# Keys of the sample caches one sequence further ahead, norm weights on the activations, and row statistics for x

## The reference, cut to what matters

```
h = x
layer 0: xn = rms_norm(h, g_norm[0]);  u, v, gate = split(xn @ w_in_a)
         v = layer_norm(v);  s = spatial(v)
         h += (u * s * silu(gate)) @ w_out_a
every layer i: h += (p[i] @ w_ple[i]) * sigmoid(rms_norm(h, g_ple[i]) @ w_ple_gate[i])
         k, v = split(rms_norm(h, g_kv) @ w_kv)
layer 1: xn = rms_norm(h, g_norm[1]);  q, gate = split(xn @ w_in_b)
         h += (stick_breaking(q, k, v and the paged cache) * silu(gate)) @ w_out_b
y = rms_norm(h, g_final)
rms_norm(x, g) = x / sqrt(mean(x * x) + eps) * g
```

## Time and profile before

| | |
|---|---|
| median of 3 runs | 1244.79 us (1242.97 to 1245.74) |
| the profiled execution, its own time | 1243.67 us |
| its span in the profile | 1241.9 us |
| mean granted TensorE clock | 0.931 of full speed |
| busy: PE, PEld, DVE, ACT, POOL | 1150.2, 1007.1, 608.0, 438.4, 358.1 us |
| HBM read, written | 103.53 MB, 6.95 MB |

### The profile page before, as it was taken

The page is one execution under the profiler, slowest core; times in us unless marked ns, Lnnn a source line. Parts: engine busy times, 40 slices in busy tenths (PEclk is TensorE's granted clock), DMA queues, the critical chain, the costliest instruction groups (busy, mean ns, idle before and its releaser), DMA issues.

```text
span 1241.9 us, 20511 instructions
## 1 busy us (share of the span) xinstructions
PE 1150.2 (93%) x7950; PEld 1007.1 (81%) x7950; DVE 608.0 (49%) x869; ACT 438.4 (35%) x685; POOL 358.1 (29%) x262
## 2 busy tenths in 40 slices
PE   7899799999999897998999999999988868799797
PEld 6899699999999897997877778787646546489796
DVE  5655445533455444555666666665443212233443
ACT  5111235431343323233455546545533212122321
POOL 6422166522365146462111111100001000005542
PEclk9999899999999998999999999999957877779899
DMA  8222122233222422213122121121315564712201
GB/s 228 83 68 84 51 69 68 85 97 94 72 68 68 120 85 68 68 52 87 51 69 69 51 66 53 51 68 34 115 46 203 176 231 172 242 53 79 68 1 72
DMA packets 148264, 111.23 MB, mean 90 GB/s; under 512 B 3970, under 2 KB 138258, under 8 KB 148114
## 3 DMA queue, kind: packets, MB, share of 16 engines
q1 hardware_dynamic: 148210, 110.49, 28.9%
HBM read 103.53 MB, written 6.95 MB: 89 GB/s over the span
## 4 chain that ended last, share of the span: by engine, by line
PE 79%; DVE 6%; SPq 4%; DMA 3%; POOL 3%; issue 2%; ACT 2%; DVEq 0%; ACTq 0%; POOLq 0%
PE acc L1127 54%; PE zb L1296 4%; PE ob L1327 4%; DMA kpage<-in_cache_k_dram 3%; PE acc L1390 2%; PE zb L1312 2%; PE zb L1315 2%; PE acc L1280 2%; SPq L558 2%; PE zb L1250 1%; PE ob L1439 1%; POOL sumsq L704 1%; POOL raw L669 1%; PE acc L1161 1%; PE zb L1299 1%
## 5 line engine op out<-in xcount | busy, mean ns | idle before, releaser
L1127 PE MATMUL acc<-act_hi,w_hi 128*128 128x272 f32 x1904 | 403.5, 293 | 17.6 <-DVE gate L1744 9.1
L1127 PE MATMUL acc<-act_hi,w_lo 128*128 128x272 f32 x1904 | 398.2, 291 | 0.0
L1127 PE MATMUL acc<-act_lo,w_hi 128*128 128x272 f32 x1904 | 397.8, 291 | 0.0
L1127 PEld LDWEIGHTS acc<-act_hi,w_hi 128*128 128x128 f32 x1904 | 304.7, 191 | 24.0 <-issue 10.2
L1127 PEld LDWEIGHTS acc<-act_lo,w_hi 128*128 128x128 f32 x1904 | 304.1, 192 | 0.0
L1127 PEld LDWEIGHTS acc<-act_hi,w_lo 128*128 128x128 f32 x1904 | 302.6, 192 | 0.0
L669 POOL TENSOR_TENSOR raw<-raw,cols 128x1024 f32<-128x1024 f32 x96 | 194.0, 2031 | 295.4 <-DMA raw<-in_w_in_b_dram 114.9
L838 ACT ACTIVATE w_hi<-raw 128x1024 fp32r<-128x1024 f32 x120 | 126.4, 1055 | 224.3 <-PE acc L1127 143.9
L1537 DVE TENSOR_TENSOR w_lo<-raw,w_hi 128x1024 fp32r<-128x1024 f32 x120 | 168.6, 1406 | 68.5 <-ACT w_hi L838 68.0
L1767 DVE TENSOR_SCALAR relz<-zb,bias 128x128 f32<-128x128 f32 (+1 forms) x64 | 35.2, 550 | 97.1 <-ACT absz L983 97.1
L983 ACT ACTIVATE absz<-zb,bias 128x128 f32<-128x128 f32 (+1 forms) x64 | 33.7, 526 | 121.4 <-PE zb L1299 121.3
(11 more groups left out here) (234 smaller groups left out, 1322.3 us busy)
## 6 DMA issues: line engine op xcount, KB each, us to landing
raw<-in_w_in_a_dram SPq DMA_DIRECT2D x48, 512.0 KB, 4.0
kpage<-in_cache_k_dram SPq DMA_DIRECT2D x32, 512.0 KB, 5.8
vpage<-in_cache_v_dram SPq DMA_DIRECT2D x32, 512.0 KB, 5.1
raw<-in_w_out_a_dram SPq DMA_DIRECT2D x16, 512.0 KB, 4.0
raw<-in_w_ple_gate_dram SPq DMA_DIRECT2D x16, 512.0 KB, 3.9
raw<-in_w_kv_dram SPq DMA_DIRECT2D x16, 512.0 KB, 3.9
raw<-in_w_in_b_dram SPq DMA_DIRECT2D x16, 512.0 KB, 4.0
raw<-in_w_out_b_dram SPq DMA_DIRECT2D x8, 512.0 KB, 5.6
```

What stands on the lines that cost most here:

```text
L1127: mm = pe.matmul(t[:, c, 0:TH], wt[:, s, kt, :], xt[:, kt, c * TH:(c + 1) * TH], start=start and kt == kts[0] and wt is w_hi and xt is xh, ...
```

## The change

Three parts.

**Sample loads.** SP now loads the keys of b before the values of b-1. Each load keeps its own wait.

**Norm weights.** `g_norm[0]` and both `g_ple` no longer multiply the panels on POOL, but the activations: ACT's `act_hi` takes a scale, DVE's `act_lo` becomes one scalar_tensor_tensor (h * g - act_hi). Only the 32 panels of `w_kv` and `w_in_b` are still scaled on POOL, since these two share one set of activations and differ in their weight; for the rest ACT waits for the DMA itself.

**Start.** The mean squares of x come from batch-norm statistics on DVE (rows of `x_nat`, mean squared plus variance), with Ln, Exp and Newton on 5 columns instead of 544. The inverse roots become diagonal matrices `diag`, which PE spreads with ones to `rinv` after the first value panel. ACT, not DVE, copies the turned x into `h`. The transposes of `ws_nat` move behind the first group of value panels.

```diff
-            for b in range(2, NB):
-                sp.wait_ge(keyed, (b - 1) * KEYS)
-                load_keys(b)
-                sp.wait_ge(v_full, (b - 1) * 2)
-                load_values(b)
+            for b in range(2, NB + 1):
+                if b < NB:
+                    sp.wait_ge(keyed, (b - 1) * KEYS)
+                    load_keys(b)
+                if b > 2:
+                    sp.wait_ge(v_full, (b - 2) * 2)
+                    load_values(b - 1)
...
+        def scaled(p):
+            return END_PL0 <= p < END_B + AHEAD
...
             for n in range(KT):
                 squares(n)
-                scale_next()
...
-                act.wait_ge(raw_scaled, panel.now(1))
+                if scaled(panel.before + panel.here):
+                    act.wait_ge(raw_scaled, panel.now(1 - END_PL0))
+                else:
+                    act.wait_ge(raw_in[s], panel.lap(SLOTS) * 16 + 16)
...
+                    nc.scalar.activation(act_hi[into][:, sl(n), :], h[:, sl(n), :], ACT.Identity,
+                                         scale=gain[:, sl(n)]).then_inc(x_hi, 1)
...
+                    dve.scalar_tensor_tensor(one(act_lo[into]), one(h), gain[:, sl(n)],
+                                             one(act_hi[into]).bitcast(F32), ALU.mult, ALU.subtract).then_inc(x_lo, 1)
...
+            for t in range(TT):
+                act.wait_ge(turned, t + 1)
+                n = P if t < QB else NS
+                nc.scalar.activation(h[:, :, tokens(t)].rearrange("p (a b) t -> p a b t", a=2),
+                                     acc[t % 2][:, :, :].rearrange("p a (b t) -> p a b t", t=P)[:, :, :, 0:n],
+                                     ACT.Copy).then_inc(h_in, 1)
+            accs.step(TT + 1)
+            split_next()
+            act.wait_ge(x_mean, 1)
+            nc.scalar.activation(ln_s[:, 1, :], ln_s[:, 0, :], ACT.Ln).then_inc(x_root, 1)
+            act.wait_ge(x_root, 1)
+            nc.scalar.activation(ln_s[:, 1, :], ln_s[:, 1, :], ACT.Exp, scale=-0.5).then_inc(x_root, 1)
...
+            value_tiles(0)
+            for half in range(2):
+                t = turn()
+                dve.tensor_copy(ws_t[:, half * (NG // 2):(half + 1) * (NG // 2), :], t[:, 0, :]).then_inc(acc_read, 1)
```

More of the change, by code:

```diff
@@ L667, in scale @@
                     pool.engine_nop().then_inc(raw_scaled, 1)
-                else:
-                    pool.tensor_tensor(raw[:, s, :, :], raw[:, s, :, :], gain[:, :, None].to_broadcast([P, KT, P]),
-                                       ALU.mult).then_inc(raw_scaled, 1)
+                    panel.step()
+                    return
+                pool.tensor_tensor(raw[:, s, :, :], raw[:, s, :, :], gain[:, :, None].to_broadcast([P, KT, P]),
+                                   ALU.mult).then_inc(raw_scaled, 1)
                 panel.step()
             def scale_next():
-                if panel.reg is None and panel.now() >= END:
-                    return
                 p = panel.before + panel.here
+                assert scaled(p)
                 if panel.reg is not None:
@@ L721, in _ @@
                 .then_inc(bs_ready, 1)
-            turns[0] = N_AV // SLOTS - 1
-            with repeat(pool, turns[0], (panel, SLOTS)):
-                for k in range(SLOTS):
-                    scale_next()
-            for k in range(SLOTS):
-                scale_next()
             pool.wait_ge(vout_step, 1)
@@ L748, in turn @@
                         pool.tensor_tensor(s_t[:, :], u_r[:, :], g_r[:, :], ALU.mult).then_inc(y_made, 1)
-                turns[0] = N_UG // SLOTS - 1
-                with repeat(pool, turns[0], (panel, SLOTS), (ytile, 2)):
+                with repeat(pool, N_UG // SLOTS, (ytile, 2)):
                     turn()
-                turn()
             mix(0)
-            for n in range(KT):
-                scale_next()
             mix(1)
@@ L770, in embed @@
                 squares(KT - 1, True)
-            embed()
+            panel.step(END_PL0)
+            embed(0)
             turns[0] = NP - 1
@@ L778, in _ @@
                     scale_next()
-            for k in range(4):
+            for _ in range(AHEAD + 1):
                 scale_next()
@@ L1555, in turn, with lo_x @@
                 return t
-            def lo_x(n, into, src=None):
+            def lo_x(n, into, src=None, gain=None):
                 xt.step()
@@ L1619, in _ @@
+            dve.scalar_tensor_tensor(ln_s[:, 0, :], ln_s[:, 0, :], EPS, mv[:, :, 1], ALU.add, ALU.add)\
+                .then_inc(x_mean, 1)
+            turns.step(TT)
+            accs.step(TT)
             t = turn()
             dve.tensor_copy(cols[:, :], t[:, 0, 0:N_COL]).then_inc(acc_read, 1)
-            lo_tokens(QB)
             split_next()
-            for half in range(2):
-                t = turn()
-                dve.tensor_copy(ws_t[:, half * (NG // 2):(half + 1) * (NG // 2), :], t[:, 0, :]).then_inc(acc_read, 1)
+            dve.wait_ge(x_root, 2)
@@ L1626, in _ @@
+            newton(ln_s[:, 1, :], ln_s[:, 0, :], ln_s[:, 2, :])
+            for c in range(TT):
+                n = P if c < QB else NS
+                ins = dve.tensor_scalar(diag[0:n, c, 0:n], ident[0:n, 0:n], ln_s[0:n, 1, c:c + 1], None, ALU.mult)
+            ins.then_inc(diag_set, 1)
+            for n in range(KT):
+                lo_x(n, 0, None, g_norm_c[0])
             for _ in range(AHEAD - 1):
                 split_next()
-            rms()
-            with repeat(dve, N_AV // SLOTS, (panel, SLOTS), (done, SLOTS), (accs, 2 * SLOTS), (turns, SLOTS)) as i:
+            dve.wait_ge(rinv_full, 1)
```

136 lines of the change are left out of this document (70 added, 66 removed).

## The result

| | before | after |
|---|---|---|
| median | 1243.88 us (1242.04 to 1245.74, 4 runs) | 1192.49 us (1191.33 to 1193.57, 4 runs) |
| span of the profiled execution | 1241.9 us | 1191.2 us |
| mean granted TensorE clock | 0.931 | 0.951 |

The changed kernel takes 0.9587 of the time, 95% interval 0.9568 to 0.9605: 51.4 us less. 1192 us was predicted.

A forecast was written before the change was run, and what follows sets the result against it. PE was taken as the bound, busy 1150.2 of 1241.9 us, with gains left only in sample steps, out-panel ends and start. 35.9 + 13.4 + 3.5 = 52.8 off 1243.67 gave 1190.9, plus 1.1 for the median: 1192 us, range 1185 to 1207.

The forecast's parts named there:

- Sample steps: Five steps from 969.33 to 1072.83 us: all five waits for keys go, steps take 13.5 us, 35.9 us less.
- The ring through SP's queue: In the sample steps: product, four loads of values, four loads of keys, transposes, product; the change takes the values out.
- The rival of a DMA bound of 14.7 us: Sample steps: loads can't overlap, steps last 14.7 us instead of 13.5, 6 us less gain, 1198 us; chance 0.15.
- Norm weights: Ends of the two out-panel stages: without POOL's scaling PE resumes earlier, twice 6.7, so 13.4 us less.
- 8.61 - 0.9: Panel after the wait at an out-panel stage's end: 8.61 us before, 0.9 us taken back, between 0 and 2.58.
- everything between the ends at nothing: Between the stages' ends, POOL's scalings lay beside PE's full stretches, so their absence was costed at nothing.
- "some 5 us" of the last part: Ends of both out-panel stages, among the signs to look for: Ln comes some 5 us after the last block.
- Start: First panel at about 17.8 us, second group at 54.0 instead of 58.50: 3.5 us less, between 0 and 6.
- loses about 1 us: Second group of value panels at the start: after the new wait for a PSUM tile, about 1 us of clock lost.
- The clock stays low in the steps: Sample steps: the waits go but the clock stays low, 21.3 us less instead of 35.9, 1207 us; chance 0.12.
- the slower case: Sample steps: PE runs at the 1.2 GHz level through all five, 25.4 us a step, 1251 us; chance 0.02.
- a full recovery at the ends: Out-panel ends: clock recovers wholly, 1.7 twice, and the start gains its upper bound, 2.5: 1186 us; chance 0.08.

The follow-up runs named there:

- loads_alone: The kernel before with only the new order of the page loads: 1206.97 us, 0.9707.
- filled_waits: The kernel before, old order of loads, with 13 extra identity matmuls on PE in each of sample steps 1 to 5, during the waits for keys: 1233.65 us, 0.9925.
- light_steps: The changed kernel with less PE work in the sample steps (half the key transposes and most cumulative sums left out from the third sequence): 1180.8 us, one run.
- copies_first: The changed kernel with DVE's two copies of ws_t moved ahead of the five statistics of the first group of values: 1185.57 us, 0.9542.
- gate_panels_alone: The kernel before with only the gate panels' norm weights moved to the activations; POOL still passes each panel on by a nop: 1232.84 us, 0.9911.
- busy_waits: copies_first plus extra identity matmuls at PE's waits at the start, in the gate stages and before the first turn of keys: 1174.6 us, 0.9449.
- busy_no_tail: busy_first_gap without the added matmuls of the last two sample steps: 1165.05 us, 0.938.
- busy_attention: busy_waits plus 20 short unused matmuls per block on PE in the prompt's last attention passes: 1172.62 us, 0.942.
- busy_tail: busy_attention plus short unused matmuls in the last two sample steps, in place of the key transposes: 1170.76 us, 0.9423.
- busy_start: The changed kernel with 14 extra identity matmuls on PE between the transposes of x and the first panel: 1192.44 us, 0.9588.
- busy_first_gap: busy_tail plus 27 more short unused matmuls in the first wait of the last attention passes: 1167.53 us, 0.9385.

## Why the prediction was right, point by point

The total was right to 0.5 us, and that close only by luck. The parts summed to 52.8 us, the spans differ by 50.7, since 2.8 us were lost and 1.6 gained in places that the sum left out, the start gave 1.3 less and the norm weights 0.5 more. Of the 2 us that this makes, the choice of runs gave 1.5 back: the forecast added 1.1 us for the median over the profiled execution, and the changed kernel's median came out 0.4 below its own profiled one.

**Sample steps: right, 35.9 against 35.8.** The ring through SP's queue was the cause, the step came out as composed from rows of before, 13.55 against 13.5, and loads_alone gave 36.3 by itself. That the clock is part of it is shown by filled_waits (about 11 us), and that the waits alone are not the price also: they were 21.3. The rule of the Trainium skill that stood beside that term ("TensorE: Matmul & The Clock Gate", section "HAM oscillation — how this bites in real kernels") holds here, in waits of 3.2 to 5.3 us with the transposes at 3.67 us or so behind each. The rival of a DMA bound of 14.7 us falls with the steps of 13.55, and light_steps has no wait for a page at a mean of 12.4.

**Norm weights: right, 13.4 against 13.9** (7.1 and 6.8). Blocks 6.01 us apart, Ln 6.1 us after the last block (471.79 to 477.85), against 6.3 in the sum (474.2 to 480.5; the "some 5 us" of the last part was loose). The panel after the wait took 7.79 us where I had 8.61 - 0.9 = 7.7; that this term fits is in part luck, since the same panel behind the same wait takes 6.25 us in three other profiles (copies_first). gate_panels_alone with 12.3 in its two stages shows that most of it, not all, is the scaling; the rest is ACT's wait for the DMA.

**Start: right in its places, wrong in one term, 3.5 against 2.2.** First panel at 17.68 (17.8), second group at 53.95 (54.0). The failed term is the clock behind the new wait, "loses about 1 us": it lost 2.6 (14.89 against 12.31). copies_first shows it: with the wait gone, both go. Two smaller terms were off and offset each other: the spread of `diag` took 1.3 us (25.80 to 27.12), not 0.6, and the gap before the second group 3.0, not some 4.

**Not foreseen: 2.8 us lost in the pair stage of layer 1.** The text cost everything between the ends at nothing. The code there is the same, but the first panel took 8.97 us instead of 7.73, and 1.5 us more lie in the last attention pass. The timelines of PE show to the instruction where, before and after:

```profile
893.85 0.70 PE L1296 MATMUL zb<-qt_t,kt_t 64*128 64x256 f32 x2 [1.84 <-ACT wts L996]
...
894.64 1.07 PE L1327 MATMUL ob<-wts,vb_nat 128*64 128x512 f32 x2
```
```profile
885.87 1.22 PE L1301 MATMUL zb<-qt_t,kt_t 64*128 64x256 f32 x2 [1.84 <-ACT wts L999]
...
887.24 1.97 PE L1332 MATMUL ob<-wts,vb_nat 128*64 128x512 f32 x2
```

Behind the same wait of 1.84 us PE was at the low level at once after the change, and some 2 us later before it; the groups behind these take the same time in both. gate_panels_alone has the same loss and loads_alone hasn't: the stage takes 396.1 to 396.4 us in all six profiles that have the norm weights on the activations and whose waits there are unfilled, and 393.5 to 393.8 in the three that haven't. So it comes with the norm weights. The panel's 1.2 us go when its wait is filled (busy_waits); the attention pass still has its 1.5 us then, and in busy_no_tail, with the pass filled as well, the whole stage takes 382.5 us (540.73 to 923.26). The clock is the cause. Why it falls sooner after this change, in code that the change doesn't touch, stays open; busy_attention and busy_tail, with the same code as busy_waits up to that wait, have 0.70 us there again.

**Not foreseen: 1.6 us gained in the step after the last keys**, which had taken 13.15 us and takes 11.51: the low clock that the waits for keys had brought reached one step further than the five that I counted. filled_waits shows it, with 11.50 us for that step.

**Slower and clock rivals.** "The clock stays low in the steps" is refuted (transposes at 1.97 and 1.92), and so is the slower case; a full recovery at the ends was not met in this profile (7.79 us for the panel, not 6.0).

## What to carry to other kernels

When loads for several buffers share one queue that stops at waits, write down for each load what it stands behind: a load that waits for an early event must not stand behind one that waits for a late one. Price a wait of PE at its length plus what the low clock costs around it, here 1.7 to 2.6 us for most waits of 2.5 to 5 us, and look at the panels behind each wait and ahead of it, new waits also. Take no difference of under 3 us from one profile as the worth of an edit before you have looked where it lies: here a stretch of low clock of 1.6 us came and went in steps that no edit touched. Where a wait can't be removed, products of no use into a free tile are worth trying, but only as long as the path isn't in PE itself, and up to the very end of the wait.

## What was not expected of the hardware

The clock fell after waits of 1.84 us (busy_tail) and 2.00 us (busy_start), and in the latter 1.3 us later, within unbroken work. In five profiles it even fell in sample steps in which PE waited 0.95 us or less at a time: steps of 15.1 to 15.2 us instead of 13.55 in busy_start, busy_attention, busy_tail and busy_first_gap, and 13.0 instead of 11.4 in light_steps, each 1.6 us longer. How long it stayed low was not the same either: behind the same gap it was back at 873.7 us in busy_tail and at 889 in busy_attention, which makes 7 us. "TensorE: Matmul & The Clock Gate" of the Trainium skill, section "HAM oscillation — how this bites in real kernels", tells of such falls behind longer waits; here shorter ones had them too.

DVE's `w_lo` took 2.26 us beside POOL's squares and 1.21 alone (the rows at 462.52 above; 457.60 us, 1.21). "SBUF — State Buffer" of the Trainium skill, section "SBUF: two separate sides", says that DVE and GpSimd take turns at a shared pair of ports for whole instructions, and the trace agrees: 1.05 us more. It costs nothing here, since the panel had 6.01 us of cover.
